# Summing attention probabilities over the key tiles on GpSimd before TensorE sums over the keys

## The reference, cut to what matters

```python
p_s = jax.nn.softmax(ss, axis=-1)          # selected keys: branch 1
o_s = p_s @ v_sel
p_w = jax.nn.softmax(jnp.where(m_w, sw, NEG), axis=-1)   # window keys: branch 2
o_w = p_w @ vwb
return gg[..., 0:1] * o_c + gg[..., 1:2] * o_s + gg[..., 2:3] * o_w
```

## Time and profile before

| | |
|---|---|
| median of 3 runs | 1926.9 us (1926.46, 1926.9, 1932.48) |
| profiled execution, from first to last instruction | 1930.2 us |
| the profiled execution's own time | not given apart from its span |
| PE busy in the span | 1909.0 us, 99% |
| DVE, ACT, POOL busy | 1384.4, 956.3, 41.7 us |
| the 8 pairs of the sparse attention | from about 832 to 993.6 us |

### The profile page before, as it was taken

How to read it: one execution, slowest core, us unless ns; L and a number is a source line. 1 busy time by engine, 2 the same in 40 slices (tenths; PEclk the granted TensorE clock), 3 DMA queues, 4 the chain that set the end, 5 groups by cost and what they waited for, 6 DMA issues and landing times.

```text
span 1930.2 us, 26942 instructions
## 1 busy us (share of the span) xinstructions
PE 1909.0 (99%) x9208; PEld 1536.0 (80%) x9208; DVE 1384.4 (72%) x2198; ACT 956.3 (50%) x1350; POOL 41.7 (2%) x51
## 2 busy tenths in 40 slices
PE   9999999999999999999999999999999999999998
PEld 9987888887777788866668888888886788888887
DVE  7986444565999876877747888863398778888534
ACT  5667433446777633667745433333366543333322
POOL 0200000001000000000000000000011000000000
PEclk9999999989999999999999999999999999999999
DMA  5220333325999625410003333323341133333332
GB/s 194 89 66 12 98 98 98 94 69 207 358 356 347 226 61 163 142 43 3 3 18 105 98 98 98 98 98 100 106 132 39 51 93 98 98 98 98 98 110 88
DMA packets 68634, 219.41 MB, mean 114 GB/s; under 512 B 11648, under 2 KB 14880, under 8 KB 68416
## 3 DMA queue, kind: packets, MB, share of 16 engines
q1 hardware_dynamic: 64240, 212.46, 33.9%
q10 hardware_dynamic: 4304, 5.77, 1.2%
HBM read 209.05 MB, written 2.10 MB: 109 GB/s over the span
## 4 chain that ended last, share of the span: by engine, by line
PE 93%; DVE 5%; ACT 1%; DMA 1%; issue 1%; SPq 0%; POOL 0%; DVEq 0%; ACTq 0%; POOLq 0%
PE psum L1140 64%; PE psum L1645 7%; PE psum L1619 2%; PE psum L1846 2%; PE psum L1556 2%; PE psum L1664 2%; PE psum L1628 1%; PE psum L1852 1%; PE psum L1312 1%; PE psum L2014 1%; PE psum L1812 1%; PE psum L1820 1%; PE psum L1549 1%; PE psum L1765 1%; DVE sig L3339 1%
## 5 line engine op out<-in xcount | busy, mean ns | idle before, releaser
L1140 PE MATMUL psum<-x_hi,w_hi 128*128 128x512 f32 (+1 forms) x1344 | 494.2, 378 | 0.0
L1140 PE MATMUL psum<-x_hi,w_lo 128*128 128x512 f32 (+1 forms) x1344 | 490.2, 375 | 0.0
L1140 PE MATMUL psum<-x_lo,w_hi 128*128 128x512 f32 (+1 forms) x1344 | 490.1, 375 | 0.0
L3062 DVE TENSOR_TENSOR w_lo<-raw,w_hi 128x1024 fp32r<-128x1024 f32 x243 | 296.3, 1221 | 187.4 <-ACT w_hi L2136 187.0
L2136 ACT ACTIVATE w_hi<-raw 128x1024 fp32r<-128x1024 f32 x243 | 256.1, 1055 | 187.8 <-DMA raw<-stream 187.2
L1140 PEld LDWEIGHTS psum<-x_hi,w_hi 128*128 128x128 f32 x1344 | 246.5, 188 | 47.5 <-issue 1.9
L1140 PEld LDWEIGHTS psum<-x_lo,w_hi 128*128 128x128 f32 x1344 | 246.5, 188 | 46.0 <-issue 1.4
L1140 PEld LDWEIGHTS psum<-x_hi,w_lo 128*128 128x128 f32 x1344 | 246.4, 188 | 45.7
L1140 PE MATMUL psum<-hid_hi,w_hi 128*128 128x512 f32 (+2 forms) x710 | 261.2, 375 | 0.5 <-DVE hid_lo L4266 0.5
L1140 PE MATMUL psum<-hid_hi,w_lo 128*128 128x512 f32 (+2 forms) x710 | 259.8, 373 | 0.0
L1140 PE MATMUL psum<-hid_lo,w_hi 128*128 128x512 f32 (+2 forms) x710 | 259.8, 373 | 0.0
(11 more groups left out here) (690 smaller groups left out, 2875.7 us busy)
## 6 DMA issues: line engine op xcount, KB each, us to landing
raw<-stream SPq DMA_DIRECT2D x251, 512.0 KB, 3.6
raw<-experts SPq DMA_DIRECT2D x70, 512.0 KB, 5.2
raw_more<-experts SPq DMA_DIRECT2D x68, 512.0 KB, 5.4
staged<-staged ACTq DMA_DIRECT2D x64, 64.0 KB, 3.3
out_fm<-resid SPq DMA_DIRECT2D x7, 256.0 KB, 2.2
resid<-x_fm SPq DMA_DIRECT2D x3, 528.0 KB, 7.2
consts<-consts_in SPq DMA_DIRECT2D x1, 1373.0 KB, 14.2
staged<-staged SPq DMA_DIRECT2D x20, 64.0 KB, 2.5
```

Of the source, the lines that this page charges most:

```text
L1140: last = pe.matmul(o, wt[:, slot, k * P:(k + 1) * P], m[part], start=start and p == 0, stop=stop and p == 2, skip_group_check=True)
L3062: dve.tensor_tensor(w_lo[:, slot, :], raw[:, slot, :], w_hi[:, slot, :].bitcast(F32), ALU.subtract)\
```

## The change

For the first 7 of the 8 pairs, GpSimd adds the exponentials of the four key tiles by query, per (branch, half), into four new buffers `probs_summed` of 512 columns (`PSUMMED`, placed in the free slots of `w_hi`). Per pair that is 16 instructions: 4 copies of 128x128 (key tile 0, the first 128 queries), 4 adds of 128x384 (tile 0 + tile 1), 4 adds of 128x128 (tile 3 into the last 128 queries) and 4 adds of 128x256 (tile 2 into the last 256). PE then sums over the keys of that one tile: four matmuls of 512 columns (`whole_sums`) after the scores of step 2 of the next pair, in place of the matmuls by ones in x = 0, 1 and 2. The last pair keeps the old way.

ACT's exponentials wait besides for the adds that read the buffer that they overwrite; GpSimd waits at a pair's start until PE has used the sums of the pair before. `keep_sums` waits for `whole_sums`, `keep_values` for the values alone. The semaphore `inv_loaded` is merged into `consts_loaded`.

```diff
-N_OUTS = 2 + len(VALUES)
+N_OUTS = 2 + len(VALUES) + 1
+N_ADDS = 16
+WIDE_ADDED, END_ADDED = {6: 5, 7: 6, 8: 8, 9: 10}, {6: 7, 7: 9, 8: 11, 9: 12}
+ADDED_BY = {**{_i - 4: _n for _i, _n in WIDE_ADDED.items()}, **END_ADDED, 10: 14, 11: 16}
+SUMS_AT = 2
...
-            sp.dma_start(inv[:, :, :], invcnt_in).then_inc(inv_loaded, 16)
+            sp.dma_start(inv[:, :, :], invcnt_in).then_inc(consts_loaded, 16)
...
+            def copy_first(p, i):
+                pool.tensor_copy(PSUMMED[i - 2][:, 0:P], probs_of(p, i)[:, 0:P]).then_inc(probs_added, 1)
+            def add_second(p, i):
+                pool.tensor_tensor(PSUMMED[i - 6][:, P:SEQ], PT[slot_of(p, i - 4)][:, P:SEQ], probs_of(p, i)[:, 0:SEQ - P], ALU.add).then_inc(probs_added, 1)
+            def add_last(p, i):
+                tail = PSUMMED[i - 6][:, SEQ - P:SEQ]
+                pool.wait_ge(probs_added, N_ADDS * p + WIDE_ADDED[i])
+                pool.tensor_tensor(tail, tail, PT[slot_of(p, i)][:, SEQ - P:SEQ], ALU.add).then_inc(probs_added, 1)
+            def add_third(p, i):
+                for half in range(2):
+                    row = 2 * (i - 10) + half
+                    tail = PSUMMED[row][:, SEQ // 2:SEQ]
+                    pool.wait_ge(probs_added, N_ADDS * p + END_ADDED[6 + row])
+                    pool.tensor_tensor(tail, tail, probs_of(p, i)[:, SEQ // 2 * half:SEQ // 2 * (half + 1)], ALU.add).then_inc(probs_added, 1)
+            for p in range(PAIRS2 - 1):
+                if p:
+                    pool.wait_ge(pv_done, N_OUTS * p)
+                for i in range(2, 6):
+                    copy_first(p, i)
+                add_second(p, 6)
+                add_second(p, 7)
+                add_last(p, 6)
+                add_second(p, 8)
+                add_last(p, 7)
+                add_second(p, 9)
+                add_last(p, 8)
+                add_last(p, 9)
+                add_third(p, 10)
+                add_third(p, 11)
...
+                if whole or x == 2:
+                    mm.then_inc(pv_done, 1)
+                if whole:
+                    return
...
+            def whole_sums(p):
+                pe.wait_ge(probs_added, N_ADDS * (p + 1))
+                for row in range(4):
+                    half, b = row // 2, 1 + row % 2
+                    mm = pe.matmul(sums_bank()[32 * row:32 * row + 32, :], VV[:, b - 1, p // 4, 0, HD:HD + 32], PSUMMED[ROW.index((b, half))][:, :],
+                                   start=True, stop=True, skip_group_check=True)
                 mm.then_inc(pv_done, 1)
...
                     later_maxima(p, i, FINDS)
+                    if i == SUMS_AT and p:
+                        whole_sums(p - 1)
...
                     act.wait_ge(pv_done, N_OUTS * q + FREES[j])
+                    if j >= 2 and q + 1 < PAIRS2:
+                        act.wait_ge(probs_added, N_ADDS * q + ADDED_BY[j])
...
-                act.wait_ge(pv_done, N_OUTS * (p + 1))
+                act.wait_ge(pv_done, N_OUTS * (p + 1) - 1)
...
-                dve.wait_ge(inv_loaded, 16)
+                dve.wait_ge(consts_loaded, 32)
```

More of the change, by code:

```diff
@@ L309, in build @@
         w_lo = nc.alloc_sbuf_tensor_at("w_lo", [P, SLOTS, UNIT], F32R, offset=raw_at)
+        w_hi_at = (nc.sbuf_base + 31) // 32 * 32
         w_hi = sb("w_hi", [P, SLOTS, UNIT], F32R)
@@ L499, in build @@
         PTR = {n: placed(f"probs_turned_hi_{n}", homes[n], [P, SEQ], F32R) for n in (0, 1, 4, 5)}
+        PSUMMED = [placed(f"probs_summed_{x}", w_hi_at + (U["wo2"] + 2 + x // 2) % SLOTS * UNIT * 4 + x % 2 * 2 * KB, [P, SEQ]) for x in range(len(ROW))]
         CEX = placed("cmp_probs_turned", x_at + 28 * KB, [P, SEQ])
@@ L546, in build @@
         x_loaded = [sem(f"x_loaded{i}") for i in range(4)]
-        inv_loaded = sem("inv_loaded")
         pairs_moved = sem("pairs_moved")
@@ L649, in build @@
         exp_done = sem("exp_done")
+        probs_added = sem("probs_added")
         pv_done = sem("pv_done")
@@ L1085, in _, with probs_of @@
             pool.memset(CHOOSE[:, :, :].bitcast(F32), 0.0).then_inc(forms_set, 1)
+            def probs_of(p, i):
+                pool.wait_ge(exp_done, N_STEPS * p + i + 1)
+                return PT[slot_of(p, i)]
+            def copy_first(p, i):
[27 more added lines that the diff above has]
+                add_third(p, 11)
             pool.wait_ge(oa_ready, PAIRS2)
@@ L1437, in _ @@
                 take_pair(r)
-                pe.wait_ge(consts_loaded, 16)
+                pe.wait_ge(consts_loaded, 32)
                 pe.wait_ge(pooled, c + 1)
@@ L1836, in values_side_by_side @@
             def values_side_by_side(p, x):
+                whole = p + 1 < PAIRS2
                 pe.wait_ge(exp_done, N_STEPS * p + VALUES_NEED[x])
@@ L1845, in values_side_by_side @@
                             i, col = PLACE[b, half, kt]
-                            pe.matmul(values_bank(b)[half * HD:(half + 1) * HD, P * kt:SEQ], VV[:, b - 1, p // 4, kt, 2 * half * HD:(2 * half + 1) * HD],
-                                      PT[slot_of(p, i)][:, col:col + SEQ - P * kt], start=kt == 0, stop=kt == 2, skip_group_check=True)
+                            mm = pe.matmul(values_bank(b)[half * HD:(half + 1) * HD, P * kt:SEQ], VV[:, b - 1, p // 4, kt, 2 * half * HD:(2 * half + 1) * HD],
+                                           PT[slot_of(p, i)][:, col:col + SEQ - P * kt], start=kt == 0, stop=kt == 2, skip_group_check=True)
+                if whole or x == 2:
+                    mm.then_inc(pv_done, 1)
+                if whole:
+                    return
                 for kt in VALUES[x]:
@@ L2366, in _ @@
                 act.activation(SELF[:, half, :], consts[:, a:a + 1].to_broadcast([P, P]), ACT.Identity, bias=consts[:, a + 1:a + 2]).then_inc(fforms_copied, 1)
-            act.wait_ge(consts_loaded, 16)
+            act.wait_ge(consts_loaded, 32)
             act.activation(IDF[:, :], ident, ACT.Copy).then_inc(fforms_copied, 1)
```

## The result

The changed kernel takes **1915.6 us** (median of 4 runs, 1915.28 to 1915.92). The kernel before, on the same chip, takes 1926.7 us (median of 4, 1926.34 to 1932.48). The medians differ by 11.1 us, and the ratio of the times is 0.9932, with a 95% interval of 0.9918 to 0.9946. So it is faster by more than 0.3%, and by more than the forecast of 8.3 us. The ratio of the two medians is 0.9943; the recorded ratio also weighs the one run of 1932.48 of before.

The account below looks back on a forecast made before the run. PE was taken to bound the kernel, busy all of each 20.10 us pair. A saving of 11.06 us less 2.8 us of stall gave -8.3 us, a median of 1918.6 us, range 1914.5 to 1927.

Parts of the forecast that it names:

- the stall of PE: PE waits for held DVE at step 10's spreads and the pair's end: 0.4 us a pair, 2.8 us in all.
- What PE is spared: Three blocks by ones go, one block of four sums comes: 1.58 us a pair, 11.06 us over 7 pairs.
- What GpSimd's adds do to DVE: DVE's two-SBUF-input instructions are held while GpSimd reads: 2.6 us of delay a pair, mostly covered by DVE's idle time.
- Find 10's read: DVE's read at step 8 ends 0.2 us late, and the two spreads of step 10 on PE wait for it.
- the first rival: Nothing stalls, as DVE's idle time takes the holding: -11.06 us, 1915.8 us; chance 0.14.
- Is GpSimd in time: GpSimd's last add before PE's new sums: done at position 20.5, 1.7 us before PE asks at 22.25.
- the dear bound: GpSimd's work a pair with wide adds at 1.34 us: 12.3 us, against 8.8 us as taken.
- the turn-taking reading: GpSimd and DVE took strict turns in the earlier trace, leaving 0.73 to 0.82 us per 384-column GpSimd instruction.
- the second rival: Dear or late GpSimd adds, or late shares, eat most of the gain: -2 us, about 1925 us; chance 0.26.
- DVE as the bound: Rival: holding makes DVE bound the pair and the kernel slower, up to +12.6 us, 1939.5 us; chance 0.12.
- ACT, SP and the constants at nothing: Later `keep_sums`, later share DMAs, ACT's new waits and the merged semaphore were taken to cost 0 us.
- The span forecast: Profiled span of 1921.9 us, from 1930.2 us before, 3.3 us above the median, less the saving.

Follow-up runs that it names:

- e3: Changed kernel with GpSimd's copies and adds cut to one column and the block of sums moved behind the 64-wide values of step 1; median 1920.0 us.
- e1: Changed kernel with GpSimd's 16 copies and adds a pair cut to one column each, all waits kept; median 1921.2 us, stage 150.75 us.
- e2: Changed kernel with each GpSimd copy and add replaced by one or two memsets, which only write SBUF; median 1919.1 us.
- e7: Changed kernel with the 128- and 256-column adds fused two in one, 12 GpSimd instructions a pair, block of sums not moved; median 1922.7 us.
- e4: Changed kernel with full adds and only the block of sums moved right behind the 64-wide values of step 1; median 1925.0 us.
- e5: Changed kernel with the block of four sums cut to one 32-column matmul from the second pair on; median 1916.0 us.
- a0_after: The changed kernel run again with nothing changed, as control; median 1918.8 us, shortest run 1915.64 us.

## Why the prediction was right in its sign and too small

The step that failed is the stall of PE, "0.4 us a pair, 2.8 us in all", which the forecast added to the bare saving; the runs show 0.2 us at the most. That the ratio puts the time 0.7 us outside the range is no more than the scatter of the runs of before.

- **What PE is spared: right in sum, by luck.** 11.06 us forecast, 10.97 measured. PE's own work gives only 9.7 us, 0.20 a pair less than forecast, for the steps between 128-wide matmuls and the 32-wide block, which were put at nothing; e3 takes 0.17 of them away. The missing 1.4 us are made up by 1.3 from elsewhere that nobody forecast. The last pair was to grow by 1.19 - 0.57 = 0.6 and shrank by 0.30, where PE had waited for ACT and DVE five times (1.8 us) and now does twice (1.2); the other 0.4 lie in pair 0 and in the one pair of 20.43, in which PE waited 0.20 us for `cmp_probs_turned` (at 942.93).
- **What GpSimd's adds do to DVE: the mechanism right, its size too large.** 2.6 us of delay a pair was forecast. DVE's busy time rose by 0.98, and 0.72 of it goes with the load (e1). The working gave each instruction that meets a working GpSimd half a wide add. But GpSimd is held in turn (its adds of 1.01 and 0.46 took 1.46 and 0.91), and with short adds between the wide ones three of the four DVE rows were held for 0.04 to 0.14 us only. That GpSimd's reading holds DVE and its writing doesn't (e2) is what the page "SBUF — State Buffer" of the Trainium skill (section "SBUF: two separate sides") says, and this case agrees by 0.684 to 0.687 us beside memsets against 1.11 beside an add. The same page gives a lock for the whole of an instruction, and e7 agrees: DVE's three rows end 0.55 to 0.56 us after the end of the add beside them, however long they were held.
- **The stall: the step that failed.** "0.4 us a pair, 2.8 us in all". e1 shows 0.2 us in all at the most. Find 10's read was taken to end 0.2 late because DVE would have been held by 0.2 ahead of it, and it was not: its read began exactly when it could. At the pair's end there was no stall either: the holding (0.71 us in the whole pair, where 2.6 was forecast) did not fill the room, and DVE still waits 1.04 us for the find at 919.73. Without that term the sum is the first rival's 1915.8 us, 0.2 from the measured 1915.6, and that near only because the two errors of 1.4 and 1.3 us above cancel.
- **Is GpSimd in time: right, but by less.** Forecast 8.8 us of work a pair and 1.7 us of room; measured 11.45 (near the dear bound of 12.3) and 0.5. The wide add alone is 1.01 us and not 0.9, above the 0.73 to 0.82 that the turn-taking reading of the earlier trace rows gave; one of 128 columns is 0.46 and not 0.37; and holding, which I charged to DVE alone, falls on GpSimd as well. e4 shows how little was missing for the second rival: asked 1.2 us earlier, PE waits up to 1.0, 0.7 on average.
- **DVE as the bound** did not come about, but e5 and e7 show it near. At 18.3 us a pair PE waits for it in two of three pairs, and another grouping of the same adds brings pairs of 20.4 us.
- **ACT, SP and the constants at nothing: right.** `keep_sums` (L2898) starts at 923.71, 0.14 behind the block's end; no wait of PE's matmuls on a DMA of the shares is in the view; the work behind the stage is 936.9 against 936.6.
- **The span forecast** (1921.9) took the 3.3 us between span and median for a constant. They were the lowered clock of one execution: its time is 1932.48, 2.3 us above its span. The forecast of the median doesn't rest on it.

Left open: why the last pair waits less than before, the rest of about 0.3 us of the stage that no wait shows, and what lowers the clock in some runs.

## What to carry to other kernels

When work goes to GpSimd that reads SBUF, price each add by a row of its own shape and count the holding on both engines; then look whether the engine that is held has room before it hands the delay on, for a held engine that was waiting anyway costs nothing. Look at the order of GpSimd's reads where the other engine has two-input work: here fewer and longer instructions, with no short ones between the wide, ended earlier on paper and made each pair 1.6 us longer. Where a producer runs beside the consumer, know the margin at the place of the first use; here 1.2 us earlier turned a gain of 11 us into one of 5.

## What the runs showed of the hardware

- GpSimd's add of 128 partitions in fp32, two inputs in SBUF: 1.01 us for 384 columns, 0.46 for 128 undisturbed, and 1.46 and 0.91 beside DVE's two-input instructions (0.45 us of holding each time). The copy of 128x128 takes 0.29.
- A block of 32-wide matmuls amid 128-wide ones costs PE 0.19 us more than its own length, and 0.17 of that went when it stood behind 64-wide ones (e3).
- The granted clock fell for short stretches in some executions and not in others. In a0_after (columns as in the windows above):

```profile
835.00:840.00 5.00, 3.48 (x18) 2.54 (x17) 4.73 (x11) 3.77 (x7) 2.27 (x5) 1.00 0.26 56
840.00:845.00 5.00, 4.75 (x18) 3.70 (x20) 2.55 (x12) 4.15 (x7) 2.11 (x4) 0.66 0.07 12
```

  PE was busy 3.48 of 5 us, and the clock was 0.66 over the next 5; the pair took 19.37 us where the same pair of the same kernel took 17.44. In before PE was busy 3.58 us in the first of these windows, and its clock stayed at 1.00 in the second. Ahead of the stretch of 0.50 in before, PE was busy 1.22 of the 2 us from 406 to 408; it was the same in the first profile of the changed kernel, where the clock did not fall. So what sets it off isn't shown. a0's five runs lie 7.9 us apart, the two longest at a mean clock of 0.994 and 0.995 (1923.54 and 1921.36 us), but one of 1918.76 has 0.999, so the clock isn't all of the scatter. It is as much as most terms of this study.
